# Moving the low halves of two split operands by 128 bytes in the on-chip memory of a two-block transformer kernel

## What is computed

```
# first block, last part
f = rms_norm(h, g_norm_ffn)
h = h + (silu(f @ w_gate) * (f @ w_up)) @ w_down        # 1024 -> 2816 -> 1024
x = rms_norm(h, g_final)
# second block, the part that reads the memory (256 tokens)
mem_h = _rmsnorm(mem, g_mem)
kv = mem_h @ w_kv                                        # 1024 -> 2 * 1024
q  = _rmsnorm(q, q_gain);  k = _rmsnorm(kv[:, :, 0], k_gain);  v = kv[:, :, 1]
o_mem = softmax(q k^T) v
```

## The kernel before

| tile | start, less the weights', modulo 256 |
|---|---|
| h_hi, h_lo | 0, 0 |
| memT_hi, memT_lo | 0, 0 |
| turned_hi, turned_lo; xgs_hi, xgs_lo (experts) | 0, 0 |
| merged_hi, merged_lo | 64, 64 |
| mixT_hi, mixT_lo | 64, 192 |
| ysT_hi, ysT_lo | 192, 64 |
| xT_hi, xT_lo; o_m, o_g, o_d (hi, lo) | 192, 192 |

## Time and profile before

### The profile page before, as it was taken

How to read it: one execution, slowest core, us unless ns; L and a number is a source line. 1 busy time by engine, 2 the same in 40 slices (tenths; PEclk the granted TensorE clock), 3 DMA queues, 4 the chain that set the end, 5 groups by cost and what they waited for, 6 DMA issues and landing times.

```text
span 1007.7 us, 16344 instructions
## 1 busy us (share of the span) xinstructions
PE 987.0 (98%) x6730; PEld 892.9 (89%) x6730; DVE 681.9 (68%) x1021; ACT 586.0 (58%) x856; POOL 45.2 (4%) x57
## 2 busy tenths in 40 slices
PE   6999999999999999999999999999999989999997
PEld 6998988999999999889898888998999978888885
DVE  5866767677555555585575766566556679998886
ACT  6574577665434343474585545776444558777773
POOL 4101000000000000010010001100000000000001
PEclk9999999999999999999999999999999989999999
DMA  9994533456565555564443334554656919999994
GB/s 260 278 308 136 169 124 126 160 174 205 174 202 177 201 178 199 185 203 161 135 165 127 124 126 126 170 170 128 189 187 209 325 52 317 365 368 372 371 369 175
DMA packets 168248, 206.31 MB, mean 205 GB/s; under 512 B 11431, under 2 KB 143118, under 8 KB 168174
## 3 DMA queue, kind: packets, MB, share of 16 engines
q1 hardware_dynamic: 159598, 196.01, 59.7%
q0 software_dynamic: 2224, 6.07, 2.0%
q10 hardware_dynamic: 6352, 3.19, 1.2%
HBM read 201.56 MB, written 4.73 MB: 205 GB/s over the span
## 4 chain that ended last, share of the span: by engine, by line
PE 91%; DMA 4%; DVE 3%; ACT 1%; issue 1%; POOL 0%; SPq 0%; DVEq 0%; ACTq 0%; POOLq 0%
PE bank L624 78%; DMA ring<-in_w_down 1%; PE bank L761 1%; PE bank L817 1%; PE bank L807 1%; DMA ring<-in_w_in 1%; DVE w_lo L600 1%; PE bank L3048 1%; PE bank L2722 1%; DMA ring<-in_w_out 1%; PE bank L2777 1%; PE bank L2739 1%; DMA x<-in_x 1%; ACT w_hi L592 0%; PE bank L3088 0%
## 5 line engine op out<-in xcount | busy, mean ns | idle before, releaser
L600 DVE TENSOR_TENSOR w_lo<-ring,w_hi 128x1024 fp32r<-128x1024 f32 (+1 forms) x302 | 423.1, 1436 | 178.3 <-ACT w_hi L592 178.0
L592 ACT ACTIVATE w_hi<-ring 128x1024 fp32r<-128x1024 f32 (+1 forms) x302 | 357.6, 1225 | 186.9 <-PE bank L624 144.5
L624 PE MATMUL bank<-xT_hi,w_hi 128*128 128x256 f32 x896 | 253.0, 282 | 0.0
L624 PE MATMUL bank<-xT_lo,w_hi 128*128 128x256 f32 x896 | 250.3, 279 | 0.0
L624 PE MATMUL bank<-xT_hi,w_lo 128*128 128x256 f32 x896 | 250.3, 279 | 0.0
L624 PEld LDWEIGHTS bank<-xT_hi,w_hi 128*128 128x128 f32 x896 | 168.7, 188 | 2.5 <-issue 1.6
L624 PEld LDWEIGHTS bank<-xT_hi,w_lo 128*128 128x128 f32 x896 | 170.1, 190 | 0.0
L624 PEld LDWEIGHTS bank<-xT_lo,w_hi 128*128 128x128 f32 x896 | 168.6, 188 | 0.8 <-issue 0.2
L624 PE MATMUL bank<-w_hi,xT_hi 128*128 128x512 f32 (+1 forms) x208 | 77.6, 373 | 0.3 <-ACT cmp_in L1313 0.3
L624 PE MATMUL bank<-w_hi,xT_lo 128*128 128x512 f32 (+1 forms) x208 | 76.1, 366 | 0.0
L624 PE MATMUL bank<-w_lo,xT_hi 128*128 128x512 f32 (+1 forms) x208 | 76.0, 365 | 0.0
(11 more groups left out here) (549 smaller groups left out, 1789.0 us busy)
## 6 DMA issues: line engine op xcount, KB each, us to landing
ring<-in_w_in SPq DMA_DIRECT2D x54, 1024.0 KB, 5.2
ring<-in_w_down SPq DMA_DIRECT2D x31, 1024.0 KB, 7.0
ring<-in_w_gate SPq DMA_DIRECT2D x40, 512.0 KB, 7.2
ring<-in_w_up SPq DMA_DIRECT2D x40, 512.0 KB, 8.8
ring<-in_w_gate SPq DMA_DIRECT2D x11, 1024.0 KB, 5.4
ring<-in_w_up SPq DMA_DIRECT2D x11, 1024.0 KB, 5.4
ring<-in_w_out SPq DMA_DIRECT2D x8, 1024.0 KB, 5.1
ring<-in_w_mem_kv SPq DMA_DIRECT2D x8, 1024.0 KB, 5.2
```

The lines of the kernel that those rows point to most:

```text
L592: act.activation(HIGHS[HI_SLOT[s]][:, k, :], RAWS[SLOT[s]][:, k, :], ACT.Copy).then_inc(w_hi_ready, 1)
L600: vec.tensor_tensor(LOWS[SLOT[s]][:, k, :], RAWS[SLOT[s]][:, k, :], HIGHS[HI_SLOT[s]][:, k, :].bitcast(F32), ALU.subtract).then_inc(w_lo_r ...
L624: ins = pe.matmul(dst, a, b, start=(start and j + m == 0), stop=(stop and j == len(pairs) - 1 and m == 2), **kw)
```

## The change

h_hi moves from 4 KB to 2 KB (the place of hT, a tile that is used much later), and h_lo from 6 KB to 4 KB and 128 bytes. memT_hi stays at 36 KB; memT_lo moves from 44 KB to 44 KB and 128 bytes. So both high parts stay at 0 from the weights modulo 256, and both low parts go from 0 to 128. No instruction, wait or transfer is added, removed or reordered.

```diff
-    h_hi, h_lo = (place((4 + 2 * i) * KB, "h_" + n, [P, 2, T], F32R) for i, n in enumerate(("hi", "lo")))
+    h_hi, h_lo = (place((2 + 2 * i) * KB + 128 * i, "h_" + n, [P, 2, T], F32R) for i, n in enumerate(("hi", "lo")))
...
-    memT_hi, memT_lo = (place((36 + 8 * i) * KB, "memT_" + n, [P, KT, T], F32R) for i, n in enumerate(("hi", "lo")))
+    memT_hi, memT_lo = (place((36 + 8 * i) * KB + 128 * i, "memT_" + n, [P, KT, T], F32R) for i, n in enumerate(("hi", "lo")))
```

## The result

The changed kernel takes 1012.68 us (median of 8 runs, 1009.77 to 1013.09) against 1009.72 us for the kernel before in the same comparison (8 runs, 1009.00 to 1011.04). The ratio is 1.0023, with a 95% interval of 1.0013 to 1.0032: slower, by a little more than the 0.2% that can be told from no change, and above the forecast's range. Two more comparisons gave 1.0038 (1.0026 to 1.0050) and 1.0027 (1.0016 to 1.0037). These ratios are estimated from all runs of a comparison and differ a little from the ratio of the two medians, which is 1.0029 here.

What follows compares the result with a forecast made beforehand. The prediction took TensorE's matmul pace as the bound. With 0 for h and -0.1 us for memT, 1009.04 became 1008.9, and 0.04 for the median of the runs gave 1009.0 us, range 1004.0 to 1011.1.

Steps and rivals of the forecast that it cites:

- What bounds the kernel: Feed-forward, 235.5 to 430 us: only TensorE's pace counts, and its gain or loss passes to the end nearly whole.
- h_lo to 128 ... I take 0: Down slabs, 88 triples of h: they stay at 680 ns, costing 0 us.
- -0.1 of memT_lo: The memory's 64 triples: moving memT_lo to 128 saves 0.1 us of a 0.3 us excess.
- both upper bounds of the text: Two steps of loss in every triple: 1.1 us for the 88 of h, 0.8 us for the 64 of memT.
- rival C: Triples of h and memT: low loads meet the stream more, two steps each, 2.0 us slower, 1011.0; chance 0.12.
- by the row that h itself gives: Down slabs: already at the lowest observed level, 680 ns a triple, with no excess to save.
- The only row at another offset: 512-wide matmuls with xT stationary at 192: 229.2 ns each, 687.5 ns a triple.
- The earlier trace: 512-wide matmuls with xgs stationary at 0, behind transposes: 231.0 ns a step, 693 ns a triple, read as two steps.
- Rival A: Gate and up slabs behind down slabs: 1056 matmuls take the faster pace, 4.6 us saved, 1004.4; chance 0.31.
- Rival B: Moved products of h and memT: low loads meet the stream less, down to -0.9 and -1.0 us, 1007.2; chance 0.06.
- Rival D: Stretch from 698.9 to 781.5 us, 720 matmuls: starting in the other phase costs 3.2 us, 1012.2; chance 0.09.

Runs made afterwards that it cites:

- both at 128: h_hi, h_lo, memT_hi and memT_lo all at 128 from the weights, against the kernel before: 1008.79 us, ratio 0.9988.
- 64, 192: h_hi at 64 and h_lo at 192 from the weights, memT as before, against the kernel before: timed 1008.45 us, ratio 0.9992.
- 192, 64: h_hi at 192 and h_lo at 64 from the weights, memT as before, against the kernel before: single run 1008.89 us.
- 192, 192: h_hi and h_lo both at 192 from the weights, memT as before, against the kernel before: single run 1009.48 us.
- delayed runs: 8 or 15 extra 512-wide matmuls ahead of the last down slab, placement of the kernel before: 1012.90 us (1.0034) and 1012.95 us (1.0036).
- h alone: h_hi at 2 KB and h_lo at 128 from the weights, memT as before, against the kernel before: 1011.92 us, ratio 1.0023.
- memT alone: memT_lo at 128 from the weights, h as before, against the kernel before: 1011.67 us, ratio 1.0021.
- xT at 0: 192 bytes left free ahead of the weights, so xT goes from 192 to 0 from them, against the kernel before: 1017.02 us, ratio 1.0073.
- 64, 64: h_hi and h_lo both at 64 from the weights, memT as before, against the kernel before: single run 1010.69 us.

## Why the prediction was wrong

**What bounds the kernel: right.** TensorE's pace in the feed-forward passes through: what the slabs of h and memT lose is there in full in the stretch up to the first matmul with o_g (1.81 us), and so is the work of 8 or 15 added matmuls.

**The step that failed: "h_lo to 128 ... I take 0", and the -0.1 of memT_lo.** The triple of h went from 680.0 to 693.4 ns, of memT to 693.7: near both upper bounds of the text (1.1 and 0.8 us; measured 1.17 and 0.64). That is rival C, "two steps in each triple", for all the triples of h and nearly all of memT. I had given it 0.12, and only a third of that past 2.0 us. I took the value "by the row that h itself gives", but that row was measured at the offset that was being left; it bears on no other. The only row at another offset, had one step. The earlier trace rows is not a level, as the text reads it: its ten steps are 235, 233, 236, 224, 231, 236, 228, 233, 231 and 226 ns, behind transposes, and the next ones are at 227; in the slab that starts at 832.76, with the same tiles and no transposes ahead, the steps from the second to the last but one are 226.7. So offset 0 costs nothing by itself, and the sum had no row at all for 128. The argument against C, "only one load of three moves", was wrong too: the 6 ns lie beside the load of the moved h_lo, but the other 7.5 beside the next load of h_hi, which hadn't moved in offset.

**The move of h by whole kilobytes: right.** Alone it changes no pace and no time (1.0001), and the writers are as before: the cast to h_hi has its median at 427 ns, the subtraction for h_lo at 693.

**Rival A: right as a mechanism, wrong for this change.** The down slab does hand a pace to the slabs behind it, and the 22 are worth the 4.6 us worked out for it (both at 128; 3.6 and 3.75 us with 64, 192 and 192, 64). With 0, 128 it doesn't happen. The argument for A, that 256-wide slabs fall to the fast pace behind a slab at 192, doesn't carry over either: with h at 192, 192 they stay at 117.8. The text's test, that a change of pattern in the down slab may change what is handed on, isn't enough: the change and 192, 192 have another pattern and hand on the slow pace.

**Rival B: wrong.** No pair of offsets tried brings a triple at 512 below 680.

**Rival D: wrong.** The gates' stretch is as before, 720 matmuls in 82.60 us, though it starts 1.8 us later.

**The sum's missing term.** C in full was priced at 1011.0, and the change came to 1012.7 to 1013.5, beyond the range. Some of that is the base: the forecast starts from 1009.08, the median of three runs, and the eight runs of before in the comparison have 1009.72. More of it is what the text left out, the stage behind: the granted clock in the router's stage and after it. The longer kinds of half clock cost 2.0 to 3.2 us there in the profiles and some 1.85 us in the times, and 25 of the 69 runs of before have them as well. A range built on paces alone, beside a median that shifts with how many runs are of a longer kind, was too narrow.

**What stays open.** Why the longer stretch comes more often with the change. The 13 delayed runs have it 6 times, with before's placement; the 54 runs of the other kernels whose paces are changed (h alone, memT alone, both at 128, 64 and 192 timed, xT at 0) have it 47 times, those that come to the router's stage earlier than before among them as well as those that come later; so neither lateness nor a part of the change is shown to be its cause. Open too is the 0.3 to 1.4 us by which the change costs more than its triples and the mix. Nor is there a rule of offsets: nothing here explains why 192, 192 costs less than 64, 64, or which offsets hand on which pace. That the weight load and the stream meet, as the prediction reads it, fits the traces but is not shown by them.

## What to carry to other kernels

In a kernel bound by TensorE, the place where a stationary operand starts against the moving one, modulo 256 bytes, is worth 0 to 7 ns a matmul here, and one tile can be better off at 0 in its 512-wide matmuls and worse in its 256-wide ones: read the spacing of starts for each pair, and try the offset, since the pace at one says nothing of another. Count what a slab hands on to the slabs behind it with its own price: both halves at 128 lose 2.4 us in their triples and win 5.0 elsewhere. And before a difference of 0.2 to 0.4% is explained, list the mean granted clock of each run (a longer stretch at the half clock was worth as much as the change), and take the effect itself from a stretch of the trace that lies ahead of the stage that varies.

## What was not expected of the hardware

- A weight load beside a stream isn't free of it: on a start address alone, the same 24 matmuls took 5.44 us (0, 0), 5.55 (0, 128) and 5.58 (128, 128). The Trainium skill ("TensorE: Matmul & The Clock Gate", "Step-by-step: what each phase is for") says that the two have read ports of their own and that the load takes nothing from the running matmul. By these runs that doesn't hold for the spacing of fp32r matmuls with a load each.
- A pace persists: 256-wide matmuls with nothing changed about them run at 113.4 or 117.8 ns for a whole slab and for 22 of them, by where the stationary tile of the slab ahead starts, and at 119.9 with their own tile at offset 0.
- One kernel's executions differ in how long TensorE is at the half clock in and behind the same stage: the three profiles of the changed kernel show 6.83, 6.83 + 3.41 and 10.24 + 3.41 us. In 17 profiles the time from the router's first matmul to the experts' last group goes with it to within 0.6 us: 144.1 to 144.6, 146.6, and 146.7 to 147.3 us.
